# Four transformer layers and two conditioned ones on one core: attention probabilities scaled by the matmul that turns them, and the turned banks copied by two engines

## The chip, the cores and the metric

The kernel runs on one core of one Trainium2 chip. Times are device microseconds (us) of one execution. TensorE appears in the rows as two lines, PE for matmuls and PEld for the loading of their stationary operand; VectorE is DVE, ScalarE is ACT, SyncE is SP.

## The reference

A sequence of 256 tokens of width 1024 goes through four layers (mixers: NSA, MoBA, a short convolution, NSA; each followed by a gated feed-forward) and then through two more layers of another kind (MLA and neighbourhood attention). All in float32. The part that matters here is masked softmax attention with 16 heads of 64:

```python
def masked_softmax(s, mask):
    s = jnp.where(mask, s.astype(jnp.float32), -jnp.inf)
    m = jnp.max(s, axis=-1, keepdims=True)
    m = jnp.where(jnp.isfinite(m), m, 0.0)
    e = jnp.where(mask, jnp.exp(s - m), 0.0)
    d = jnp.sum(e, axis=-1, keepdims=True)
    return e / jnp.where(d > 0, d, 1.0)
...
o = (gates[:, :, 0, :, :, None] * o_cmp + gates[:, :, 1, :, :, None] * o_slc
     + gates[:, :, 2, :, :, None] * o_win).astype(h.dtype)
```

In NSA each head has a compressed, a selected and a window branch, each multiplied by a gate per token and head. With 256 tokens the selected and the window branch are both plain causal attention. MoBA is plain causal attention here, without gates.

## The kernel before, in words

Each engine runs its own instruction list, written out stage by stage in the order of `PROGRAM`; engines meet only at semaphores. Three stages use `pair_attention` with causal masks: `nsa0` and `nsa1` (16 items each: 8 tiles of two heads, times two branches) and `moba0` (8 items). A fourth, `na0`, uses the same function with 512 wide rows. An item is two heads (e = 0, 1), each with 256 query tokens in two blocks: 128 queries against 128 keys, and 128 queries against 256 keys. So a head has 384 columns (`WIDTH`), an item 768.

What one item goes through, with the engine that does it:

- scores: PE, L482, stationary and moving operand from `qk`, heads e = 0 and 1 in the two halves of the rows of the array (64 partitions each); semaphore `s_ready`.
- mask and row maximum: DVE, L2197, four instructions from `ps` to `p_pair` (part of `hid_f`); `s_taken`.
- exp with row sum: ACT, L1385, four instructions in place; `exp_done`.
- `normalize`: DVE, reciprocal of the four sums (L2172), in NSA times the gate (L2176), then the four blocks of `p_pair` times their factor (L2182); `p_ready`.
- turning: PE, L801, 12 transposes of half a block each (64 queries by 128 keys), again in the two halves of the rows, into the two banks `PAIR_T` = 4 and 5, one for each half r; `t_ready`.
- copy to `t_pair`: ACT, L1398, one instruction over both banks; `t_taken`.
- product with the values: PE, L818, stationary `v_sb`, moving `t_pair`; in NSA the first branch of a tile also takes the compressed branch from `v_sb` (its own scores and scaling are made elsewhere); `pv_done`.
- after a tile's last item: ACT (L1405) and DVE (L1792) split the result into `a_both`.

PE's list in round i of the loop holds scores(i), the turning of item i-2, the value product of item i-3. DVE's holds the maximum of item i, `normalize` of item i-1, the split of item i-4. ACT's holds exp of item i, the copy of item i-1, the split of item i-3. There is one pair of banks `PAIR_T`: the turning of an item waits until the item before it has been copied out. In the last rounds PE fills in parts of the output projection (`out_part`) around the last two turnings.

Of the kernel before, what the change touches and what calls it, by code (L numbers as in the profile page):

```python
# [13 lines left out]
P = 128  # L14
# [3 lines left out]
HD = 64  # L18
# [113 lines left out]
def program(nc, weights, small, x_t, c_rows, ctx_t, na_bias, na_bv, out_t):  # L132
    with ExitStack() as ctx:
# [4 lines left out]
        def sb(name, shape, dt=F32):  # L138
            return ctx.enter_context(nc.sbuf_tensor(name, shape, dt))
# [37 lines left out]
        low_stat = sb("low_stat", [P, 2, 4])  # L177
        cmp_max = sb("cmp_max", [P, 2 * HEADS])
        cmp_sum = sb("cmp_sum", [P, 2 * HEADS])

        q_sb, k_sb = qk[:, 0:KD], qk[:, KD:2 * KD]
        sq_sum = p_ring[:, 0, 0:S]
# [60 lines left out]
        def wait(eng, s, n):  # L243

            if n > 0:
                eng.wait_ge(s, n)
# [126 lines left out]
        p_slot = [hid_f32[0][:, 2 * S * j:2 * S * (j + 1)] for j in range(4)]  # L373
        WIDTH = {"nsa0": 3 * P, "nsa1": 3 * P, "moba0": 3 * P, "na0": 4 * P}
        PAIR_SLOTS = 3

        def p_pair(name, i):

            w = 2 * WIDTH[name]
            at = 0 if name == "na0" else FT * S - PAIR_SLOTS * w  # L380
            return hid_f32[0][:, at + i % PAIR_SLOTS * w:at + (i % PAIR_SLOTS + 1) * w]

        def t_pair(name, i):

            w = 2 * WIDTH[name]
            at = 0 if name == "na0" else FT * S - PAIR_SLOTS * w
            return hid_f32[1][:, at + i % PAIR_SLOTS * w:at + (i % PAIR_SLOTS + 1) * w]

        NEG_SCALE = {"nsa0": -HD ** -0.5, "nsa1": -HD ** -0.5, "moba0": -HD ** -0.5,
                     "mla0": -float(np.float32((NOPE + ROPE) ** -0.5)), "na0": -1.0}  # L390
# [86 lines left out]
        def _(pe):  # L477
# [283 lines left out]
            def pair_attention(name, src, beside):  # L761

                a, items = att[name], ITEMS[name]
                N, W = len(items), WIDTH[name]
                out = {}

                def out_part(tiles):
                    if not out:
                        pe.wait_ge(a["s_taken"], N - 1)
                        out["unit"], out["made"] = start_unit("AA")  # L770
                        for bank, p, _ in out["made"]:
                            start_product("A", p)
                    for k in tiles:
                        pe.wait_ge(a["o_ready"], k + 1)
                        for j, (bank, p, (ready, _)) in enumerate(out["made"]):
                            last = fm_tile(ps[:, bank, 0:S], out["unit"] % SLOTS, j * KD + k, src[k], k == 0, k == KD - 1)
                            if k == KD - 1:
                                last.then_inc(ready, 1)

                wait(pe, taken["A"], cnt.n["A"])  # L780
                for i in range(N + 3):
                    if i < N:
                        if i >= 2:
                            pe.wait_ge(a["s_taken"], i - 1)
                        for c in range(len(items[i]["heads"][0]["scores"])):
                            many = len(items[i]["heads"][0]["scores"][c][1])
                            for t in range(many):
                                for e in range(2):
                                    cols, terms = items[i]["heads"][e]["scores"][c]
                                    last = mm(ps[:, PAIR_S[i % 2][e], cols], *terms[t], t == 0, t == many - 1)  # L790
                        last.then_inc(a["s_ready"], 1)
                    beside(i)
                    if i == N:
                        out_part(range(0, 3))
                    b = i - 2
                    if 0 <= b < N:
                        pe.wait_ge(a["p_ready"], b + 1)
                        wait(pe, a["t_taken"], b)
                        for at in range(0, 2 * W, P):
                            for r in range(2):  # L800
                                last = nc.tensor.transpose(ps[:, PAIR_T[r], at // 2:at // 2 + HD], p_pair(name, b)[half(r), at:at + P],  # L801
                                                           ident[half(r), half(r)])
                        last.then_inc(a["t_ready"], 1)
                    if i == N + 1:
                        out_part(range(3, 5))
                    b = i - 3
                    if 0 <= b < N:
                        it = items[b]
                        o = PAIR_O[it["tile"] % 2]
                        pe.wait_ge(a["t_taken"], b + 1)  # L810
                        if it["tile"] >= 2:
                            pe.wait_ge(a["o_ready"], it["tile"] - 1)
                        many = len(it["heads"][0]["pv"])
                        for j in range(many):
                            for e in range(2):
                                v, t, q = it["heads"][e]["pv"][j]
                                moving = t_pair(name, b)[:, e * W + t.start:e * W + t.stop] if isinstance(t, slice) else t
                                last = nc.tensor.matmul(ps[half(e), o, q], v, moving, start=it["first"] and j == 0,  # L818
                                                        stop=j == many - 1, skip_group_check=True)
                        last.then_inc(a["pv_done"], 1)  # L820
                out_part(range(5, KD))
# [349 lines left out]
        def _(act):  # L1171
# [201 lines left out]
            def pair_attention(name, beside=None, behind=None, load_bias=None):  # L1373

                a, items = att[name], ITEMS[name]
                N, W = len(items), WIDTH[name]
                for i in range(N + 3):
                    if i < N:
                        act.wait_ge(a["s_taken"], i + 1)
                        rows = items[i]["rows"]  # L1380
                        for e in range(2):
                            for r, (c, _) in enumerate(rows):
                                at = p_pair(name, i)[:, e * W + c.start:e * W + c.stop]
                                x = len(rows) * e + r
                                last = nc.scalar.activation(at, at, ACT.Exp, bias=negmax[:, i % 4, x:x + 1], scale=-1.0,  # L1385
                                                            accum_out=sums[:, i % 4, x:x + 1])
                        last.then_inc(a["exp_done"], 1)
                        if load_bias and i + 2 < N:
                            load_bias(i + 2)
                    if beside:  # L1390
                        beside(i)
                    b = i - 1
                    if 0 <= b < N:
                        act.wait_ge(a["t_ready"], b + 1)
                        if b >= PAIR_SLOTS:
                            act.wait_ge(a["pv_done"], b - PAIR_SLOTS + 1)
                        turned = ps[:, PAIR_T[0]:PAIR_T[1] + 1, 0:W].rearrange("p r (n c) -> p r n c", c=HD)
                        nc.scalar.copy(t_pair(name, b).rearrange("p (n r c) -> p r n c", r=2, c=HD), turned).then_inc(a["t_taken"], 1)  # L1398
                    if behind:
                        behind(i)  # L1400
                    b = i - 3
                    if 0 <= b and items[b]["last"]:
                        act.wait_ge(a["pv_done"], b + 1)
                        t = items[b]["tile"]
                        nc.scalar.copy(a_hi[:, t, LAT], ps[:, PAIR_O[t % 2], 0:S]).then_inc(a["o_hi"], 1)  # L1405
# [372 lines left out]
        def _(dve):  # L1778
# [383 lines left out]
            def pair_attention(name, out_unit, beside=None, bias=False):  # L2162
# [4 lines left out]
                def normalize(b):  # L2167
# [5 lines left out]
                    if g is not None:  # L2173
                        sync()
                        both = recip[:, b % 4, :].rearrange("p (e r) -> p e r", e=2)
                        step(v.tensor_tensor(both, both, gate[:, :, g:g + REP + 1:REP].rearrange("p r e -> p e r"), ALU.mult))  # L2176
                    sync()
                    for e in range(2):
                        for r, (c, _) in enumerate(rows):
                            at = p_pair(name, b)[:, e * W + c.start:e * W + c.stop]  # L2180
                            x = len(rows) * e + r
                            last = v.tensor_scalar(at, at, recip[:, b % 4, x:x + 1], None, ALU.mult)  # L2182
                    last.then_inc(a["p_ready"], 1)

                for i in range(N + 4):
# [18 lines left out]
                        normalize(1)  # L2204
                    if beside:
                        beside(i)
                    b = i - 4
                    if 0 <= b and items[b]["last"]:
                        tiles += 1
# [53 lines left out]
            def run_nsa(j):  # L2263
                s = nsa[j]
                if cnt.n["unit"] == 0:
# [8 lines left out]
                        add_square()  # L2274
                    dve.wait_ge(rest_loaded, 16)
                    split(1)
                norm_row()
                v_rep = [h.rearrange("p (m g r c) -> p m g r c", m=2, g=GROUPS, r=REP) for h in (vg_hi, vg_lo)]
                blocks = blk_f.rearrange("p (kv l g c) -> p kv l g c", kv=2, l=16, g=GROUPS)
# [735 lines left out]
```

## Time and profile before

| | |
|---|---|
| median of 3 runs | 2270.99 us (2268.38 to 2271.54) |
| the profiled execution's own time | 2267.76 us |
| its span in the trace | 2266.0 us |
| granted TensorE clock, mean | 0.993 |
| PE busy | 2211.7 us (98%) |
| DVE busy | 1786.1 us (79%) |
| ACT busy | 1161.0 us (51%) |

The span runs from the first to the last instruction in the trace; the own time holds 1.8 us around it. A granted clock of 1.00 is 2.4 GHz, 0.50 is 1.2 GHz. Busy shares are means over stages that differ much: the three stages in question take about 0.1 ms of the 2.27.

### The profile page before, as it was taken

The numbers are of one execution on the slowest core, as the hardware profiler recorded it, in microseconds if no ns is written. First come the engines' busy times: TensorE is split into PE (matmuls) and PEld (weight loads), VectorE is DVE, ScalarE is ACT, GpSimd is POOL, SyncE is SP. The second block draws the span as 40 slices with busy tenths as digits, with TensorE's granted clock in tenths as the row PEclk, the third lists the DMA queues.
The fourth block names the chain that finished last, engine by engine and source line by source line (L and its number), as shares of the span: only waits on it lengthen the run. The fifth ranks groups of instructions, "written<-read, shape, count | busy, mean of one in ns | idle before, by whom it ended". The sixth has DMA issues, their size and how long they took to land.

```text
span 2266.0 us, 38094 instructions
## 1 busy us (share of the span) xinstructions
PE 2211.7 (98%) x15324; PEld 1975.1 (87%) x15324; DVE 1786.1 (79%) x3510; ACT 1161.0 (51%) x2042; POOL 0.2 (0%) x4
## 2 busy tenths in 40 slices
PE   7999999999999999999999999999999999999998
PEld 7878889898889988897988887788888889979998
DVE  7788977789887898878798866577877876478888
ACT  4685554665553555458655634534122235476433
POOL 0000000000000000000000000000000000000000
PEclk9999999999999999999999999999999999999999
DMA  7325656356555565650565532023454522334563
GB/s 247 135 71 218 234 198 220 122 196 235 197 209 187 195 234 197 214 207 30 205 232 200 181 112 93 1 75 130 167 187 157 176 75 103 140 104 149 207 227 125
DMA packets 70160, 373.60 MB, mean 165 GB/s; under 512 B 7392, under 2 KB 16736, under 8 KB 37984
## 3 DMA queue, kind: packets, MB, share of 16 engines
q1 hardware_dynamic: 61472, 361.52, 44.4%
q10 hardware_dynamic: 8512, 9.63, 1.4%
q8 instruction: 122, 2.00, 0.3%
q14 instruction: 54, 0.44, 0.1%
HBM read 369.03 MB, written 1.05 MB: 163 GB/s over the span
## 4 chain that ended last, share of the span: by engine, by line
PE 83%; DVE 10%; ACT 3%; DMA 2%; issue 1%; DVEq 0%; ACTq 0%
PE ps L482 80%; DVE w_lo L1792 3%; DMA w_raw<-weights 1%; DVE hid_f L2197 1%; DVE hid_f L2182 1%; PE ps L818 1%; PE ps L735 1%; ACT w_hi L1183 1%; PE ps L801 1%; ACT hid_f L1385 1%; DMA sm<-small 1%; DVE v_sb L2297 0%; DVE ps L1826 0%; DVE hid_both L1792 0%; DVE a_both L1792 0%
## 5 line engine op out<-in xcount | busy, mean ns | idle before, releaser
L482 PE MATMUL ps<-a_both,w_hi 128*128 128x256 f32 (+1 forms) x4864 | 1187.2, 330 | 16.2 <-DVE a_both L1849 10.4
L482 PEld LDWEIGHTS ps<-a_both,w_hi 128*128 128x128 f32 x4864 | 808.5, 190 | 93.5 <-issue 15.2
L482 PE MATMUL ps<-a_both,w_lo 128*128 128x256 f32 (+1 forms) x3136 | 886.2, 291 | 0.0
L1792 DVE TENSOR_TENSOR w_lo<-w_raw,w_hi 128x1024 fp32r<-128x1024 f32 (+1 forms) x632 | 707.4, 1147 | 83.8 <-ACT w_hi L1183 77.0
L482 PEld LDWEIGHTS ps<-a_both,w_lo 128*128 128x128 f32 x3136 | 595.4, 190 | 26.5
L482 PE MATMUL ps<-hid_both,w_hi 128*128 128x512 f32 (+2 forms) x2216 | 600.5, 350 | 6.2 <-DVE hid_both L1792 2.3
L1183 ACT CAST w_hi<-w_raw 128x1024 fp32r<-128x1024 f32 (+1 forms) x448 | 414.7, 974 | 369.8 <-DMA w_raw<-weights 369.0
L482 PEld LDWEIGHTS ps<-hid_both,w_hi 128*128 128x128 f32 x2216 | 385.8, 189 | 63.9 <-issue 4.6
L482 PE MATMUL ps<-hid_both,w_lo 128*128 128x256 f32 (+2 forms) x1460 | 438.4, 304 | 0.0
L482 PEld LDWEIGHTS ps<-hid_both,w_lo 128*128 128x128 f32 x1460 | 276.5, 189 | 14.3
L1189 ACT CAST w_hi<-w_raw 128x1024 fp32r<-128x1024 f32 (+2 forms) x184 | 187.8, 1021 | 1.2 <-DMA w_raw<-weights 1.2
L1826 DVE CUSTOM_DVE_ANT_1 ps<-pe_sb,X 128x1024 f32<-128x1024 f32 x104 | 127.8, 1229 | 1.8
L1548 ACT COPY p_ring<-ps 128x512 f32<-128x512 f32 x88 | 51.7, 587 | 140.0 <-PE ps L482 135.7
L1205 ACT ACTIVATE p_ring<-ps 128x512 f32<-128x512 f32 (+1 forms) x56 | 28.2, 505 | 166.9 <-PE ps L482 166.6
L1826 DVE CUSTOM_DVE_ANT_0 ps<-pe_sb,c_late 128x1024 f32<-128x1024 f32 x88 | 108.2, 1230 | 3.2
L1385 ACT ACTIVATE hid_f<-hid_f,negmax 128x128 f32<-128x128 f32 (+1 forms) x192 | 94.1, 499 | 14.1 <-DVE negmax L2197 14.1
L482 PE MATMUL ps<-w_hi,a_both 128*128 128x256 f32 x512 | 95.8, 289 | 0.0
L2490 DVE TENSOR_TENSOR p_ring<-ps,p_ring 128x512 f32<-128x512 f32 x88 | 60.6, 689 | 42.3 <-ACT p_ring L1548 42.3
L482 PEld LDWEIGHTS ps<-w_hi,a_both 128*128 128x128 f32 x512 | 81.6, 196 | 2.9 <-issue 2.5
L1792 DVE TENSOR_TENSOR hid_both<-t_ring,hid_both 128x256 fp32r<-128x256 f32 (+1 forms) x152 | 72.2, 477 | 3.2 <-ACT hid_both L1694 1.3
L482 PE MATMUL ps<-w_lo,a_both 128*128 128x256 f32 x256 | 73.3, 286 | 0.0
L1551 ACT ACTIVATE p_ring<-p_ring 128x256 f32<-128x256 f32 x88 | 36.8, 419 | 54.7 <-DVE p_ring L2492 54.6
(235 smaller groups left out, 1907.3 us busy)
## 6 DMA issues: line engine op xcount, KB each, us to landing
w_raw<-weights SPq DMA_DIRECT2D x250, 1024.0 KB, 4.6
pe_sb<-weights SPq DMA_DIRECT2D x96, 512.0 KB, 5.4
w_raw<-weights SPq DMA_DIRECT2D x64, 704.0 KB, 3.8
pe_sb<-na_bias ACTq DMA_DIRECT2D x32, 128.0 KB, 2.2
X<-x_t SPq DMA_DIRECT2D x2, 512.0 KB, 6.8
X<-c_rows ACTq DMA_DIRECT2D x2, 512.0 KB, 4.4
qk<-qk ACTq DMA_DIRECT2D x4, 256.0 KB, 6.8
qk<-ctx_t ACTq DMA_DIRECT2D x1, 1024.0 KB, 5.7
```

The source lines that it names most:

```text
L482: return nc.tensor.matmul(out, stationary, moving, start=start, stop=stop)
L735: last = nc.tensor.matmul(ps[:, o, q], v, t_ring[:, e, t], start=j == 0, stop=j == len(it["pv"]) - 1, skip_group_check=True)
L801: last = nc.tensor.transpose(ps[:, PAIR_T[r], at // 2:at // 2 + HD], p_pair(name, b)[half(r), at:at + P], ident[half(r), half(r)])
L1183: nc.scalar.copy(w_hi[:, u % SLOTS, c], raw(u, c)).then_inc(hi_split, 1)
L1189: nc.scalar.copy(w_hi[:, u % SLOTS, c], raw(u, c)).then_inc(hi_split, 1)
L1205: nc.scalar.activation(dst, src, func or ACT.Copy, **kw).then_inc(taken[ring], 1)
L1385: last = nc.scalar.activation(at, at, ACT.Exp, bias=negmax[:, i % 4, x:x + 1], scale=-1.0, accum_out=sums[:, i % 4, x:x + 1])
L1548: nc.scalar.copy(low_slot, ps[:, at, S:2 * S]).then_inc(low_copied, 1)
L1551: nc.scalar.activation(gate_sum, gate_sum, ACT.Silu).then_inc(silu_done, 1)
L1792: return v.tensor_tensor(out, a, b.bitcast(F32), ALU.subtract)
L1826: v.tensor_tensor_reduce(products, ada_w[:, a % 2, :].rearrange("p (a b) -> p a b", b=S), c, 1.0, 0.0, ALU.mult, ALU.add, mod[:, a, s_:s_ ...
L2490: v.tensor_tensor(both, ps[:, made[0][0]:made[1][0] + 1, 0:S], low_slot, ALU.add).then_inc(taken["A"], 1)
```

## The change

For `nsa0`, `nsa1` and `moba0` (not for `na0` and `mla0`) DVE no longer multiplies the probabilities by their factors. It writes four 64 by 64 diagonal matrices, one for each block of the item, into `factor` (a view of `t_ring`, four items deep), and PE multiplies by these in place of the identity: `nc.tensor.transpose` with `ident` becomes an ordinary float32 `matmul` with `factor` as the moving operand. `ident_half` holds the two diagonal blocks of the identity side by side as one 128 by 64 tile and is made once, at the start. The copy out of `PAIR_T` is split: ACT takes bank 4, DVE takes bank 5, and `t_taken` counts two for each item.

```diff
+        ident_half = sb("ident_half", [P, HD])
...
+        SCALED_TURN = ("nsa0", "nsa1", "moba0")
+        factor = t_ring.rearrange("p a (b x c) -> p (a b) x c", b=2, c=HD)
+
+        def copies(name):
+            return 2 if name in SCALED_TURN else 1
...
+        def turned(name, i, halves_of):
+
+            tokens = t_pair(name, i).rearrange("p (n r c) -> p r n c", r=2, c=HD)[:, halves_of]
+            first = PAIR_T[0] + halves_of.start
+            return tokens, ps[:, first:first + halves_of.stop - halves_of.start, 0:WIDTH[name]].rearrange("p r (n c) -> p r n c", c=HD)
...
                         pe.wait_ge(a["p_ready"], b + 1)
-                        wait(pe, a["t_taken"], b)
+                        wait(pe, a["t_taken"], copies(name) * b)
                         for at in range(0, 2 * W, P):
+                            x = 2 * (at // W) + (at % W > 0)
                             for r in range(2):
-                                last = nc.tensor.transpose(ps[:, PAIR_T[r], at // 2:at // 2 + HD], p_pair(name, b)[half(r), at:at + P],
-                                                           ident[half(r), half(r)])
+                                to, frm = ps[:, PAIR_T[r], at // 2:at // 2 + HD], p_pair(name, b)[half(r), at:at + P]
+                                if name in SCALED_TURN:
+                                    last = mm(to, frm, factor[half(r), b % 4, x, :], True, True)
+                                else:
+                                    last = nc.tensor.transpose(to, frm, ident[half(r), half(r)])
...
-                        turned = ps[:, PAIR_T[0]:PAIR_T[1] + 1, 0:W].rearrange("p r (n c) -> p r n c", c=HD)
-                        nc.scalar.copy(t_pair(name, b).rearrange("p (n r c) -> p r n c", r=2, c=HD), turned).then_inc(a["t_taken"], 1)
+                        nc.scalar.copy(*turned(name, b, slice(0, 3 - copies(name)))).then_inc(a["t_taken"], 1)
...
                     sync()
+                    if name in SCALED_TURN:
+                        v.tensor_tensor(factor[:, b % 4], ident_half[:, :].unsqueeze(1).to_broadcast([P, w, HD]),
+                                        recip[:, b % 4, 0:w].unsqueeze(2).to_broadcast([P, w, HD]), ALU.mult).then_inc(a["p_ready"], 1)
+                        return
...
+                    b = i - 2
+                    if name in SCALED_TURN and 0 <= b < N:
+                        dve.wait_ge(a["t_ready"], b + 1)
+                        if b >= PAIR_SLOTS:
+                            dve.wait_ge(a["pv_done"], b - PAIR_SLOTS + 1)
+                        v.tensor_copy(*turned(name, b, slice(1, 2))).then_inc(a["t_taken"], 1)
```

On PE, in the first rounds of `nsa0`, before the change (`sm` holds `ident`, `hid_f` is `p_pair`; an x12 row is one item's turning):

```order
L482 MATMUL ps<-qk 128x128 x2
L482 MATMUL ps<-qk 128x256 x2
L801 MATMUL ps<-sm,hid_f_0_50 128x64 x12
L818 MATMUL ps<-hid_f_1_51,v_sb 64x256 x2
L818 MATMUL ps<-hid_f_1_51,v_sb 64x128 x2
```

and after it, where the number, the shapes and the order of the matmuls are the same, and the moving operand of the twelve is `t_ring` (`factor`):

```order
L494 MATMUL ps<-qk 128x128 x2
L494 MATMUL ps<-qk 128x256 x2
L494 MATMUL ps<-t_ring,hid_f_0_50 128x64 x12
L834 MATMUL ps<-hid_f_1_51,v_sb 64x256 x2
L834 MATMUL ps<-hid_f_1_51,v_sb 64x128 x2
```

On DVE, in the same rounds of `nsa0`, before the change:

```order
L2172 RECIPROCAL recip<-sums 128x4
L2176 TENSOR_TENSOR recip<-recip,gate 128x4
L2182 TENSOR_SCALAR hid_f_0_50<-hid_f_0_50,recip 128x128
L2182 TENSOR_SCALAR hid_f_0_50<-hid_f_0_50,recip 128x256
L2182 TENSOR_SCALAR hid_f_0_50<-hid_f_0_50,recip 128x128
L2182 TENSOR_SCALAR hid_f_0_50<-hid_f_0_50,recip 128x256
L2197 ISA hid_f_0_50,negmax<-ps,sm 128x128
```

and after it, where one wide product stands in place of the four scalings, and behind it the copy of the item before (`ps` bank 5 to `t_pair`), ahead of the next item's maximum:

```order
L2187 RECIPROCAL recip<-sums 128x4
L2191 TENSOR_TENSOR recip<-recip,gate 128x4
L2194 TENSOR_TENSOR t_ring<-ident_half,recip 128x256
L2231 COPY hid_f_1_51<-ps 128x6x64
L2216 ISA hid_f_0_50,negmax<-ps,sm 128x128
```

## Rows read from the trace of the kernel before

**Rows 1.** The page: busy time of the engines, and the longest chain by line.

```profile
PE 2211.7 (98%) x15324; PEld 1975.1 (87%) x15324; DVE 1786.1 (79%) x3510; ACT 1161.0 (51%) x2042; POOL 0.2 (0%) x4
PE ps L482 80%; DVE w_lo L1792 3%; DMA w_raw<-weights 1%; DVE hid_f L2197 1%; DVE hid_f L2182 1%; PE ps L818 1%; PE ps L735 1%; ACT w_hi L1183 1%; PE ps L801 1%; ACT hid_f L1385 1%; DMA sm<-small 1%; DVE v_sb L2297 0%; DVE ps L1826 0%; DVE hid_both L1792 0%; DVE a_both L1792 0%
```

**Rows 2.** Window, `nsa0`: length; PE, PEld, DVE, ACT, POOL busy; PEclk; DMA.

```profile
122.76:128.08 5.32, 4.71 (x64) 3.23 (x61) 5.17 (x30) 5.28 (x21) 0.00 (x0) 1.00 0.03 6
```

**Rows 3.** Timeline of PEld, `nsa0`: start, length (us), instruction, [idle before <-releaser].

```profile
130.94 0.45 PEld L801 LDWEIGHTS ps<-sm,hid_f 64*128 64x128 f32 x12 [1.01 <-DVE hid_f L2182]
131.46 0.20 PEld L818 LDWEIGHTS ps<-v_sb 128*64 128x64 f32 x4
...
132.69 0.52 PEld L482 LDWEIGHTS ps<-qk 64*128 64x128 f32 x8 [0.17 <-issue]
133.38 0.46 PEld L801 LDWEIGHTS ps<-sm,hid_f 64*128 64x128 f32 x12 [0.17 <-DVE hid_f L2182]
133.91 0.63 PEld L818 LDWEIGHTS ps<-hid_f,v_sb 128*64 128x64 f32 x8
134.71 0.52 PEld L482 LDWEIGHTS ps<-qk 64*128 64x128 f32 x8 [0.17 <-issue]
136.25 0.46 PEld L801 LDWEIGHTS ps<-sm,hid_f 64*128 64x128 f32 x12 [1.02 <-DVE hid_f L2182]
```

**Rows 4.** Timeline of DVE, `nsa0`, from one item's normalisation to the next item.

```profile
131.91 0.17 DVE L2172 RECIPROCAL recip<-sums 128x4 f32<-128x4 f32 x1
...
132.32 1.01 DVE L2182 TENSOR_SCALAR hid_f<-hid_f,recip 128x128 f32<-128x128 f32 x4
133.24 0.42 DVE L1792 TENSOR_TENSOR a_both<-ps,a_both 128x256 fp32r<-128x256 f32 x1
```

**Rows 5.** Groups of instructions by form, DVE and ACT: busy us, mean ns.

```profile
L2492 DVE TENSOR_TENSOR p_ring<-p_ring,r_row 128x256 f32<-128x256 f32 x88 | 37.4, 425 | 3.0
L2758 DVE COPY qk<-ps 128x512 f32<-128x512 f32 x8 | 5.5, 688 | 6.5 <-PE ps L482 6.5
L1398 ACT COPY hid_f<-ps 128x768 f32<-128x768 f32 x40 | 31.6, 791 | 6.9 <-PE ps L801 6.6
L1548 ACT COPY p_ring<-ps 128x512 f32<-128x512 f32 x88 | 51.7, 587 | 140.0 <-PE ps L482 135.7 <-issue 4.4
```

**Rows 6.** PEld: L801 by source; L482 by form; a timeline stretch before `nsa0`.

```profile
L801 PEld LDWEIGHTS ps<-sm,hid_f x736: 134/139/227, 101.8 to 2036.7; 64*128 64x128 f32 x184
...
L482 PEld LDWEIGHTS ps<-qk 64*128 64x128 f32 x320 | 22.2, 196 | 5.9 <-issue 4.8
...
85.81 2.87 PEld L482 LDWEIGHTS ps<-k_cmp,qk 128*128 128x128 f32 x25
```

**Rows 7.** Timeline of PEld: third turning and start of `out_part`, `nsa0`, `nsa1`, `moba0`.

```profile
107.25 0.45 PEld L801 LDWEIGHTS ps<-sm,hid_f 64*128 64x128 f32 x12 [1.47 <-DVE hid_f L2182]
...
138.01 0.30 PEld L482 LDWEIGHTS ps<-a_both,w_hi 128*128 128x128 f32 x2 [0.17 <-issue]
...
1040.45 0.45 PEld L801 LDWEIGHTS ps<-sm,hid_f 64*128 64x128 f32 x12 [1.47 <-DVE hid_f L2182]
...
1071.20 0.30 PEld L482 LDWEIGHTS ps<-a_both,w_hi 128*128 128x128 f32 x2 [0.17 <-issue]
...
435.62 0.45 PEld L801 LDWEIGHTS ps<-sm,hid_f 64*128 64x128 f32 x12 [2.21 <-DVE hid_f L2182]
...
445.20 0.30 PEld L482 LDWEIGHTS ps<-a_both,w_hi 128*128 128x128 f32 x2 [0.17 <-issue]
```

**Rows 8.** Windows, `moba0` and behind the compressed scores; a turning in `moba0`.

```profile
434.00:436.00 2.00, 0.38 (x12) 0.38 (x12) 1.62 (x8) 2.00 (x8) 0.00 (x0) 1.00 0.00 0
...
438.00:440.00 2.00, 2.00 (x20) 1.37 (x18) 1.67 (x12) 2.00 (x9) 0.00 (x0) 0.50 0.04 8
...
90.00:92.00 2.00, 2.00 (x10) 1.28 (x11) 1.93 (x7) 1.54 (x2) 0.00 (x0) 0.50 0.00 0
...
438.07 0.98 PEld L801 LDWEIGHTS ps<-sm,hid_f 64*128 64x128 f32 x12 [0.20 <-DVE hid_f L2182]
```

More of the change, by code:

```diff
@@ L809, in pair_attention @@
                         o = PAIR_O[it["tile"] % 2]
-                        pe.wait_ge(a["t_taken"], b + 1)
+                        pe.wait_ge(a["t_taken"], copies(name) * (b + 1))
                         if it["tile"] >= 2:
@@ L2276, in run_nsa @@
                     split(1)
+                    step(v.tensor_tensor(ident_half[:, :], ident[:, 0:HD], ident[:, HD:P], ALU.add))
                 norm_row()
```

## The prediction

> **What bounds the kernel now.** I read the page first. PE is busy 98% of the span and the chain of waits lies on its line L482 for 80% [rows 1], so whatever lengthens PE's list outside a wait lengthens the kernel; the change can gain only where PE waits. The causal attention stages are such places. The windows over one tile of `nsa0` (two items) show why: of 5.32 us ACT is busy 5.28, DVE 5.17, PE by its records 4.71, and PEld 3.23 [rows 2]. DVE and ACT set the pace together there, and PE waits for DVE's scaling.
>
> The timeline of PEld shows how much. I measure a group from its first weight load to the first load of the next group. A turning takes 131.46 − 130.94 = 0.52 us, a value product with the compressed branch 132.69 − 131.46 = 1.23, one without 134.71 − 133.91 = 0.80, an item's scores 133.38 − 132.69 = 0.69 [rows 3]. Two items are 2 × 0.69 + 2 × 0.52 + 1.23 + 0.80 = 4.45 us of PE's list. The tile takes 136.25 − 130.94 = 5.31 [rows 3], so PE waits 0.86 a tile, 0.43 an item. That is all the room the turning has to grow in before PE sets the pace.
>
> **What DVE and ACT save.** Before, DVE's four scalings hold it from 132.32 to 133.24, 0.92 us [rows 4]. In their place stands one product of 128x256: 425 ns in the nearest row [rows 5], some 0.35 if the next instruction starts inside its tail, as DVE's do here (four scalings of 1.01 us in all let the next begin after 0.92). New is the copy of one bank, 384 columns: a DVE copy of 512 takes 688 ns, and 256 columns take 425 in the product above, halfway 0.55 [rows 5], about 0.48 with the tail overlapped. DVE: 0.92 − 0.83 = 0.09 us less an item. ACT's copy of 768 columns takes 791 ns and one of 512 takes 587 [rows 5]; 0.8 ns a column makes 0.48 for 384, so ACT saves 0.31 an item. `ident_half` costs one 64 wide DVE instruction at the start, at most 0.3 us, beside PE's matmuls on loaded weights. If PE had kept its turning at 0.52, DVE's saving would be the whole gain: 40 items × 0.09 = 3.6 us.
>
> **What PE pays.** The twelve turnings are now ordinary float32 matmuls, and the trace has none that loads 64 rows by 128 columns and streams 64 columns, so I price it by neighbours. A transpose leaves one record (40 items × 12 + 16 × 16 = 736, and L801 has x736), with a load of 139 ns [rows 6]. A float32 matmul leaves two: 40 items × 4 score matmuls are 160, and the rows show x320, with loads of 196 ns [rows 6]. So there are twice the passes, each with a longer load. The distance between passes: in the transposes six pairs (the two row halves run side by side) start within 0.45 − 0.14 us, 0.062 a pair. In the scores four pairs start their loads within 0.52 − 0.19, 0.11 a pair [rows 3, 6]. Those stream 128 and 256 columns, so the 0.11 might be streaming; but the compressed scores stream only 32 columns per 128x128 load, and 25 of their loads take 2.87 us, (2.87 − 0.19) / 24 = 0.112 apart [rows 6]. So a float32 pass costs 0.112 us when little is streamed: the load sets it. The item now has 12 pairs instead of 6: first load to last load grows from 0.31 to 11 × 0.112 = 1.23, so the turning goes from 0.52 to **1.44 us, +0.92**, over twice the 0.43 that PE has free.
>
> In the Trainium skill, TensorE: Matmul & The Clock Gate, section Terms, the transpose mode is said to be 4 times faster for float32. Four times the 0.31 us between first and last load would be 1.24; the page speaks against this change as my rows do, by the same size.
>
> Bounds of the turning. Below: 24 loads at the transposes' spacing, 12 × 0.062, would make +0.37. Above: if the two halves no longer ran side by side, 24 × 0.112 would make +2.2. The scores have the same operand type and the same halves, and run side by side; I take 0.92.
>
> **The sum.** With 1.44 a tile of NSA is 2 × 0.69 + 2 × 1.44 + 2.03 = 6.29 us of PE's list, against 4.97 to 5.15 of DVE and 4.7 of ACT: PE sets the pace and waits for nobody. From the third turning to `out_part` there were 138.01 − 107.25 = 30.76 us in `nsa0` and 1071.20 − 1040.45 = 30.75 in `nsa1` [rows 7]. PE's list in it: 12 turnings, 6 + 6 value products, 11 scores. That is 12 × 1.44 + 6 × 2.03 + 11 × 0.69 = 37.05, **+6.3**. The first two turnings add 1.84, of which the 1.47 us wait before the third [rows 7] takes up most: **+0.4**. The last two stand between full projection matmuls: 2 × 0.92 = **+1.8**. Each NSA stage +8.5, two of them +17.0.
>
> `moba0` has 8 items and no compressed branch: from the third turning to `out_part` 445.20 − 435.62 = 9.58 us [rows 7], and afterwards 4 × 1.44 + 4 × 0.80 + 3 × 0.69 = 11.03, +1.45. The 2.21 us wait before the third turning [rows 7] hides the first two. The last two add 1.84. Together **+3.3**. In the old trace the clock fell to 1.2 GHz here after PE had been busy 0.38 of 2 us [rows 8]; with longer turnings that gap nearly closes, so I count full clock; 9.58 includes what the fall cost.
>
> Sum: 17.0 + 3.3 = +20.3. Nothing later takes it back, since PE is the bound in the stages behind [rows 1]. Against the profiled execution's 2267.76 this is 2288.1; against the median of the runs shown (2270.99) it is 2291.3. I say **2290**, own range 2284 to 2298.
>
> **The rivals.**
>
> *The turning is cheap (ends on the other side).* If the passes of these 64 column matmuls kept the transposes' spacing of 0.062, a turning would be 0.89 and PE's tile 5.19 against DVE's 5.15. The whole effect in the steady part is then DVE's −0.09 an item, and the first rounds lose the 0.6 us by which `p_ready` comes earlier: at best −3.6 − 1.5 = −5, 2263 to 2266. It decides at a turning of (5.31 − 3.41) / 2 = 0.95 us: above that PE is slower than the old pace. For it speaks only that no row has just this shape; against it the spacing of 0.112 with 32 columns. Chance 0.04 for faster by over 0.2% (4.5 us, about what a measurement can tell from no change), 0.06 for no difference.
>
> *Both copies are late.* A turning now waits for ACT's and DVE's copy of the item before, and DVE's stands behind `normalize`. From the start of a turning: scores visible after 0.2, maximum of four blocks about 1.2, reciprocal and gate 0.4 (131.91 to 132.32 [rows 4]), factors 0.42, copy 0.55: 2.8 us. PE comes back to the next turning after 1.44 + 0.80 + 0.69 = 2.93. A margin of 0.15 in the items without compressed branch; if something in it is 0.3 longer, some 20 items wait 0.2 to 0.3: +5, 2295. Chance 0.13.
>
> *The clock falls.* In the rows of `moba0` the fall came after idling, and at 0.50 the loads of a turning spread over 0.98 us instead of 0.45 [rows 3, 8]. The new turning keeps the array loaded but streams in half the time only. Should a fall of 4 us, as in `moba0`, come once in each stage, it costs 2 us each, 2296; if the clock stays at 1.2 GHz through the three stages, 40 items cost some 3 us more each, 2400. For it: the clock is also at 0.50 at 90 us, right behind the compressed scores with their many loads and little streaming, though PE was busy throughout [rows 6, 8]. Against: PE's share of streaming an item hardly changes, since 0.43 of wait is replaced by 0.92 of half streaming. Chance 0.13, mostly for the small form. By the Trainium skill (the same page, Part 4: PE-mode transpose) transposes do not count as busy time for the clock; by that rule the clock in `moba0` would stay up.
>
> *Mine,* PE pays 0.92 a turning: 0.64.
>
> **How the numbers follow.** The upper rivals up to 2300 or so are taken in; below I go to where the turning costs 0.6 more in place of 0.92 (20 − 40 × 0.3 = +8). Range 2278 to 2306. Slower by over 0.2%: 0.64 + 0.13 + 0.13 = 0.90; same 0.06; faster 0.04.
>
> **What the new profile would show.** Twice the records of the turnings (960 beside 256 transposes), loads near 190 ns, 1.4 to 1.5 us from the first load to the next group; tiles of NSA 6.3 us apart; PE's idle before turnings near nothing; DVE and ACT idle some 1 us a tile, waiting for PE's scores. `out_part` of `nsa0` starts 6 to 7 us later than 138.01. I am wrong if the turnings take under 0.95, if PE still idles before them for DVE's copy, or if the windows of the three stages show a clock below 1.00 where it was 1.00.

## The result and the profile after

The changed kernel takes 2292.93 us (median of 4 runs, 2292.10 to 2293.59), the kernel before 2271.26 (4 runs, 2268.38 to 2271.81): a ratio of 1.0097, 95% interval 1.0085 to 1.0109. It is slower by 21.7 us. The profiled execution took 2292.41, with a span of 2290.3 (before 2267.76 and 2266.0).

The page after, busy time and the longest chain by line, beside [rows 1] (L494 is the matmul helper that was L482, L834 the value product that was L818):

```profile
PE 2246.6 (98%) x15804; PEld 2016.7 (88%) x15804; DVE 1785.0 (78%) x3431; ACT 1150.9 (50%) x2042; POOL 0.2 (0%) x4
PE ps L494 83%; DVE w_lo L1807 3%; PE ps L834 2%; DMA w_raw<-weights 2%; PE ps L747 1%; ACT w_hi L1199 1%; DMA sm<-small 1%; PE ps L818 0%; DVE v_sb L2323 0%; DVE hid_both L1807 0%; DVE X L1933 0%; PE ps L735 0%; DVE X L2080 0%; ACT p_ring L1337 0%; DVE X L1929 0%
```

PE has 480 records and 35 us more, DVE 79 instructions less. Of DVE's lines in the stages, L2182 and L2197 in the chain before, none stands in it now. Over one tile of `nsa0`, two items (the window's columns are those of [rows 2]):

```profile
120.86:127.17 6.31, 6.31 (x86) 5.31 (x84) 5.03 (x28) 4.74 (x19) 0.00 (x0) 1.00 0.01 3
```

The tile takes 6.31 us instead of 5.32, PE is busy in all of it, and DVE and ACT are both below their old 5.17 and 5.28. PEld's timeline over a tile shows what the time goes to, beside [rows 3]:

```profile
128.95 1.52 PEld L494 LDWEIGHTS ps<-t_ring,hid_f 64*128 64x128 f32 x24
130.54 0.63 PEld L834 LDWEIGHTS ps<-hid_f,v_sb 128*64 128x64 f32 x8
131.34 0.52 PEld L494 LDWEIGHTS ps<-qk 64*128 64x128 f32 x8 [0.17 <-issue]
131.91 1.50 PEld L494 LDWEIGHTS ps<-t_ring,hid_f 64*128 64x128 f32 x24
133.48 0.20 PEld L834 LDWEIGHTS ps<-v_sb 128*64 128x64 f32 x4
133.75 0.79 PEld L834 LDWEIGHTS ps<-hid_f,v_sb 128*64 128x64 f32 x8
134.72 0.52 PEld L494 LDWEIGHTS ps<-qk 64*128 64x128 f32 x8 [0.17 <-issue]
```

A turning has 24 loads in place of 12 and takes 1.59 and 1.57 us to the next group; the value products stand at 0.80 and 1.24 as before; the scores take 0.57. No row of the tile waits for DVE or ACT. Groups by form (busy us, mean ns | idle before and its releaser), beside [rows 5, 6]:

```profile
L494 PEld LDWEIGHTS ps<-t_ring,hid_f 64*128 64x128 f32 x960 | 59.4, 188 | 4.5 <-issue 2.7
L2231 DVE COPY hid_f<-ps 128x384 f32<-128x384 f32 x40 | 22.1, 553 | 6.2 <-PE ps L494 6.0
L1413 ACT COPY hid_f<-ps 128x384 f32<-128x384 f32 x40 | 19.1, 478 | 38.3 <-PE ps L494 38.2
L2194 DVE TENSOR_TENSOR t_ring<-ident_half,recip 128x256 f32<-128x256 f32 x40 | 17.0, 425 | 1.4
```

And the waits from 110 to 147 us (us in total, times, longest): now the other engines wait for PE.

```profile
ACT hid_f L1413 <- PE ps L494: 9.7, 12, 1.1
DVE hid_f L2216 <- PE ps L494: 7.1, 12, 0.8
```

The third turning, `out_part` and the last two turnings of `nsa0`, and the third turning and `out_part` of `moba0`, beside [rows 7]:

```profile
110.01 1.52 PEld L494 LDWEIGHTS ps<-t_ring,hid_f 64*128 64x128 f32 x24
...
147.34 0.30 PEld L494 LDWEIGHTS ps<-a_both,w_hi 128*128 128x128 f32 x2 [0.17 <-issue]
...
149.68 1.42 PEld L494 LDWEIGHTS ps<-t_ring,hid_f 64*128 64x128 f32 x24
151.17 0.63 PEld L834 LDWEIGHTS ps<-hid_f,v_sb 128*64 128x64 f32 x8
151.97 1.44 PEld L494 LDWEIGHTS ps<-t_ring,hid_f 64*128 64x128 f32 x24 [0.17 <-issue]
...
446.49 0.29 PEld L494 LDWEIGHTS ps<-t_ring,hid_f 64*128 64x128 f32 x3 [0.40 <-issue]
...
457.63 0.30 PEld L494 LDWEIGHTS ps<-a_both,w_hi 128*128 128x128 f32 x2 [0.17 <-issue]
```

From the third turning to `out_part` `nsa0` took 37.33 us (30.76 before) and `moba0` 11.14 (9.58). From the first matmul of a stage's first turning to its last value product, by the trace's records, the stages `nsa0`, `moba0`, `nsa1` went from 43.76, 22.78, 43.75 to 52.23, 26.09, 52.29: +8.47, +3.31, +8.54, together **+20.3 us**. I call this difference the stage sum below. It is read from one execution of each kernel.

### The profile page after: what moved, and what is told of

Same layout as the page of the kernel before. It is cut to its first block, busy times and chain, and to the rows that moved or that the text cites. A ratio compares the mean times of both kernels' runs of the same rounds, so it can differ in the third digit from the quotient of the medians.

```text
span 2290.3 us, 39006 instructions
## 1 busy us (share of the span) xinstructions
PE 2246.6 (98%) x15804; PEld 2016.7 (88%) x15804; DVE 1785.0 (78%) x3431; ACT 1150.9 (50%) x2042; POOL 0.2 (0%) x4
## 4 chain that ended last, share of the span: by engine, by line
PE 87%; DVE 7%; DMA 3%; ACT 3%; issue 1%; ACTq 0%; DVEq 0%
PE ps L494 83%; DVE w_lo L1807 3%; PE ps L834 2%; DMA w_raw<-weights 2%; PE ps L747 1%; ACT w_hi L1199 1%; DMA sm<-small 1%; PE ps L818 0%; DVE v_sb L2323 0%; DVE hid_both L1807 0%; DVE X L1933 0%; PE ps L735 0%; DVE X L2080 0%; ACT p_ring L1337 0%; DVE X L1929 0%
## 5 line engine op out<-in xcount | busy, mean ns | idle before, releaser
L494 PE MATMUL ps<-a_both,w_hi 128*128 128x256 f32 (+1 forms) x4864 | 1188.2, 330 | 18.4 <-DVE a_both L1864 10.5
L494 PEld LDWEIGHTS ps<-a_both,w_hi 128*128 128x128 f32 x4864 | 808.9, 190 | 96.3 <-issue 15.3
L494 PE MATMUL ps<-a_both,w_lo 128*128 128x256 f32 (+1 forms) x3136 | 886.4, 291 | 0.0
L494 PEld LDWEIGHTS ps<-a_both,w_lo 128*128 128x128 f32 x3136 | 595.8, 190 | 26.5
L494 PE MATMUL ps<-hid_both,w_hi 128*128 128x512 f32 (+2 forms) x2216 | 602.3, 351 | 6.0 <-DVE hid_both L1807 2.3
L494 PEld LDWEIGHTS ps<-hid_both,w_hi 128*128 128x128 f32 x2216 | 387.1, 190 | 64.1 <-issue 4.6
L494 PE MATMUL ps<-hid_both,w_lo 128*128 128x256 f32 (+2 forms) x1460 | 439.1, 304 | 0.0
L494 PEld LDWEIGHTS ps<-hid_both,w_lo 128*128 128x128 f32 x1460 | 277.2, 190 | 14.3
L494 PE MATMUL ps<-w_hi,a_both 128*128 128x256 f32 x512 | 95.8, 289 | 0.0
L494 PEld LDWEIGHTS ps<-w_hi,a_both 128*128 128x128 f32 x512 | 81.7, 196 | 2.9 <-issue 2.5
L494 PE MATMUL ps<-w_lo,a_both 128*128 128x256 f32 x256 | 73.3, 286 | 0.0
```

The costliest lines, as they stand in the source:

```text
L494: return nc.tensor.matmul(out, stationary, moving, start=start, stop=stop)
```

## Why the spans differ by 4 us more than the stages

The spans differ by 24.3. Part of the rest is there before the change can act: the first turning of `nsa0` starts at 104.33 instead of 101.77. The windows ahead of it, of the changed kernel:

```profile
86.00:88.00 2.00, 2.00 (x14) 1.91 (x13) 0.00 (x0) 1.21 (x3) 0.00 (x0) 0.67 0.36 53
88.00:90.00 2.00, 2.00 (x11) 2.00 (x11) 1.75 (x2) 1.16 (x2) 0.00 (x0) 0.50 0.88 344
```

And of the kernel before:

```profile
86.00:88.00 2.00, 2.00 (x20) 2.00 (x19) 0.62 (x1) 2.00 (x4) 0.00 (x0) 1.00 0.72 205
88.00:90.00 2.00, 2.00 (x15) 2.00 (x14) 2.00 (x3) 0.29 (x1) 0.00 (x0) 0.69 0.76 320
```

The granted clock falls to 0.50 in the compressed scores in both, in one execution about 2 us earlier. That is scatter and not the change: e9 and e12 below are one and the same kernel, and their first turnings start at 103.93 and 102.00. The other experiments that have PE's instructions of before up to this point start at 101.96 (e3), 102.11 (e8) and 103.75 (e2).

Another 1.5 us comes behind the three stages. The same group of loads stands at 2066.02 us before and at 2088.82 after, 22.8 later; right behind it the changed kernel's trace has the clock down, where the kernel before has 1.00, and from there on it is 24.3 behind:

```profile
2066.02 0.97 PEld L482 LDWEIGHTS ps<-sm,p_ring 128*128 128x128 f32 x8 [0.53 <-issue]
...
2088.82 0.97 PEld L494 LDWEIGHTS ps<-sm,p_ring 128*128 128x128 f32 x8 [0.53 <-issue]
...
2090.00:2092.00 2.00, 2.00 (x11) 1.95 (x11) 1.94 (x2) 0.98 (x2) 0.00 (x0) 0.57 0.04 8
```

The trace of e3 has this fall too and that of e1 has not, so it doesn't go with the turning's mode either. The medians differ by 21.7, so 1.4 us beyond the stage sum are left, which is within that scatter.

## The experiments

Each is compared with the kernel before, run beside it on the same chip (2271.5 us for e1 to e4, 2271.9 for e5 to e7, 2271.25 for e8 to e11); stage sums are differences from the one trace of the kernel before. T is a turning in `nsa0`, first load to the next group's.

**e1: the mode alone.** Only the instruction of the turning is changed in the kernel before; scaling and copy stay.

```diff
-    last = nc.tensor.transpose(ps[...], p_pair(name, b)[half(r), at:at + P], ident[half(r), half(r)])
+    to, frm = ps[...], p_pair(name, b)[half(r), at:at + P]
+    if name != "na0":
+        last = mm(to, frm, ident[half(r), half(r)], True, True)
+    else:
+        last = nc.tensor.transpose(to, frm, ident[half(r), half(r)])
```

> The kernel before, with the transposes of the three causal stages replaced by ordinary float32 matmuls by the same identity; DVE scales and ACT copies both banks as before. If the passes on PE are the whole cost: turning 1.5 to 1.6 us, NSA tiles 6.3 us apart, +20 us (2291), within 3 us of the changed kernel. If the cost came from the copy behind normalize in DVE's list or from the factors, this kernel stays within 4 us of the kernel before.

Measured 2294.38 against 2271.5, 1.0103 (1.0089 to 1.0117). PEld's timeline of e1:

```profile
121.69 1.52 PEld L482 LDWEIGHTS ps<-sm,hid_f 64*128 64x128 f32 x24
123.28 0.63 PEld L821 LDWEIGHTS ps<-hid_f,v_sb 128*64 128x64 f32 x8
...
128.00 0.19 PEld L482 LDWEIGHTS ps<-sm,hid_f 64*128 64x128 f32 x2
```

The tile is again 128.00 − 121.69 = 6.31 and the stage sum +21.8. The whole cost is the mode of twelve instructions an item. Diagonal and second copy add nothing to it; by the stage sums they take off 1.5 us, which the two medians can't tell.

**e2: transposes, twice.** In the kernel before the twelve transposes of an item are issued twice (the same result again): T grows without the mode.

```diff
+    if name != "na0":
+        for at in range(0, 2 * W, P):
+            for r in range(2):
+                to, frm = ps[...], p_pair(name, b)[half(r), at:at + P]
+                last = nc.tensor.transpose(to, frm, ident[half(r), half(r)])
```

> The kernel before, with each item of the three stages turned twice over into the same banks by transposes. As many array passes as in the changed kernel, at the transposes' spacing of 0.062 us a pair: turning 0.52 + 0.37 = 0.89, PE's tile 5.19, under DVE's and ACT's 5.3. If PE's wait of 0.43 an item is free room: nothing in the steady part, 2 x 0.37 us at the end of each stage, +2 us (2273). If the number of passes counts, not the load of each: +20. If the cost is simply additive on PE: 40 x 0.37 = +15.

Measured 2277.86, 1.0030 (1.0019 to 1.0041), stage sum +6.8: the 2273 that I gave for free room was too low, and the +15 of a plain addition too high. The timeline of e2 over one tile shows why (PE's, DVE's and PEld's rows that matter; L2202 is the maximum, L2187 the scaling, L802 and L807 the two halves of the turning):

```profile
125.18 0.52 PEld L482 LDWEIGHTS ps<-qk 64*128 64x128 f32 x8 [0.17 <-issue]
...
126.15 0.29 DVE L2202 CUSTOM_DVE_ANT_0 hid_f<-ps,sm 128x128 f32<-128x128 f32 x1 [0.39 <-PE ps L482]
...
127.68 1.01 DVE L2187 TENSOR_SCALAR hid_f<-hid_f,recip 128x128 f32<-128x128 f32 x4
...
128.74 0.45 PEld L802 LDWEIGHTS ps<-sm,hid_f 64*128 64x128 f32 x12 [0.63 <-DVE hid_f L2187]
...
129.63 0.20 PEld L823 LDWEIGHTS ps<-v_sb 128*64 128x64 f32 x4
...
130.86 0.52 PEld L482 LDWEIGHTS ps<-qk 64*128 64x128 f32 x8 [0.17 <-issue]
```

DVE waits for PE's scores, and PE then waits for DVE's scaling, which stands behind that maximum. That is a loop over the engines. It takes two items, one tile, to come round: the scores of item i release its maximum; behind this in DVE's list stands the scaling of item i − 1, which releases that item's turning; behind the turning in PE's list come the value product of item i − 2, with the compressed branch, and the scores of item i + 2. In the rows: scores to maximum 126.15 − 125.18 = 0.97, maximum to turning 128.74 − 126.15 = 2.59, the turning 0.89, value product with the compressed branch 130.86 − 129.63 = 1.23; together 5.68. Only one of the tile's two turnings is in it. Without the turning it is **4.79 + T**, and with the old T of 0.52 that is 5.31, the tile of before. The sum from scores to scores is the tile by construction; that the rest stays at 4.79 while T changes, and that the loop can be cut, is what e3 and e8 have to show.

**e3: half the turning as plain matmuls.**

```diff
+    if name != "na0" and at < W:
+        last = mm(to, frm, ident[half(r), half(r)], True, True)
```

> The kernel before, with head e = 0 turned by ordinary float32 matmuls by the identity and head e = 1 by transposes: half the dose. Turning 0.52 + 6 x 0.112 - 3 x 0.062 = 1.01, PE's tile 5.43 against 5.31. With free room of 0.43 an item: +0.06 an item in NSA, nothing steady in MoBA, 2 x 0.49 at the end of each stage: +4.5 us (2276). A cost in proportion to the dose: +10 (2281).

Measured 2280.39, 1.0044 (1.0031 to 1.0056), stage sum +9.0, where a cost in proportion to the dose was foreseen at +10 and free room at +4.5. PEld's timeline of e3 (L805 is the half left as transposes):

```profile
121.52 0.75 PEld L482 LDWEIGHTS ps<-sm,hid_f 64*128 64x128 f32 x12 [0.57 <-DVE hid_f L2185]
...
127.31 0.75 PEld L482 LDWEIGHTS ps<-sm,hid_f 64*128 64x128 f32 x12 [0.58 <-DVE hid_f L2185]
127.92 0.33 PEld L805 LDWEIGHTS ps<-sm,hid_f 64*128 64x128 f32 x6
128.32 0.20 PEld L821 LDWEIGHTS ps<-v_sb 128*64 128x64 f32 x4
```

T is 1.01, the tile 5.79; 4.79 + 1.01 is 5.80. PE still waits 0.57 a tile for DVE, though the tile has grown: the wait was not free room.

**e4: the changed kernel, transposes again.** Factors and second copy stay, but the turning doesn't apply the factors, so the probabilities are left unscaled.

```diff
-    last = mm(to, frm, factor[half(r), b % 4, x, :], True, True)
+    last = nc.tensor.transpose(to, frm, ident[half(r), half(r)])
```

> The changed kernel, with the transposes by the identity put back; DVE still writes the factors, which nobody uses, so the probabilities stay unscaled, and both engines copy a bank each. It gives what the change would save if turning cost nothing more. From the sum: DVE -0.09 an item and the first rounds shorter, -4 to -5 us (2266). If splitting the copy brings waits of its own (both copies late), it is at or above the kernel before.

Measured 2267.21, 0.9983 (0.9974 to 0.9992), stage sum −3.4. DVE's saving is real, by the interval 2 to 6 us. The NSA stages gain 0.7 each, in their first rounds, `moba0` 2.0. In `moba0` part of this can be the clock: only the trace of the kernel before has it at 0.50 there. PEld's timeline of e4:

```profile
122.46 0.48 PEld L816 LDWEIGHTS ps<-sm,hid_f 64*128 64x128 f32 x12 [0.95 <-DVE t_ring L2194]
123.01 0.20 PEld L834 LDWEIGHTS ps<-v_sb 128*64 128x64 f32 x4
...
127.75 0.48 PEld L816 LDWEIGHTS ps<-sm,hid_f 64*128 64x128 f32 x12 [0.95 <-DVE t_ring L2194]
```

The tile is still 5.29: PE now waits for the product that makes the factors, which has the scaling's place in the loop, with a T of 0.55 in the waiting item.

**e5: the second copy without the rest.** The kernel before, with the turned ones copied in two halves as after (ACT bank 4, DVE bank 5), but the scaling on DVE and the transposes as before.

```diff
+    b = i - 2
+    if name in SCALED_TURN and 0 <= b < N:
+        dve.wait_ge(a["t_ready"], b + 1)
...
+        v.tensor_copy(*turned(name, b, slice(1, 2))).then_inc(a["t_taken"], 1)
```

> The kernel before, with only the copy split: ACT bank 4, DVE bank 5, scalings left on DVE and transposes as before. DVE's tile goes from 5.17 to 5.17 + 2 x 0.48 = 6.13 us: +0.4 an item, +14 to +17 us (2286). If DVE had room in its list, or if ACT's shorter copy set the pace, no change or a gain.

Measured 2281.57, 1.0044 (1.0032 to 1.0056), stage sum +10.7. The tile was foreseen at 5.17 + 2 × 0.48 = 6.13 and is 128.19 − 122.06:

```profile
122.06 0.48 PEld L812 LDWEIGHTS ps<-sm,hid_f 64*128 64x128 f32 x12 [0.60 <-DVE hid_f L2192]
...
125.29 0.48 PEld L812 LDWEIGHTS ps<-sm,hid_f 64*128 64x128 f32 x12 [1.36 <-DVE hid_f L2192]
...
128.19 0.23 PEld L812 LDWEIGHTS ps<-sm,hid_f 64*128 64x128 f32 x4 [0.60 <-DVE hid_f L2192]
```

DVE's list is nearly full in that tile (5.99 of 6.13 us busy). The total, 2286, was foreseen too high, as I counted all 40 items at that pace; of the 16 turnings of an NSA stage only the 12 between the third and `out_part`, six tiles, run at it (6 × 0.82 = 4.9, and the stage grew by 4.9).

**e6: the changed kernel with both copies on ACT.**

```diff
-    return 2 if name in SCALED_TURN else 1
+    return 1
...
-    if name in SCALED_TURN and 0 <= b < N:
+    if copies(name) == 2 and 0 <= b < N:
```

> The changed kernel, with ACT copying both banks as before. If PE's list is the whole bound, the same as the changed kernel within 2 us, NSA tiles 6.3 us apart. If DVE's copy just before the next turning holds PE back, this is 3 to 5 us faster than the changed kernel.

Measured 2294.89 against 2271.9, 1.0100 (1.0087 to 1.0113). The tile is 6.32 by the turnings at 120.42 and 126.74, the stage sum +21.3. DVE rid of its copy changes nothing, so no late copy sets the pace. In the changed kernel itself DVE's copy is done only 0.11 us before PE's next turning at 131.91 (timeline of DVE):

```profile
130.90 0.42 DVE L2194 TENSOR_TENSOR t_ring<-ident_half,recip 128x256 f32<-128x256 f32 x1
131.25 0.55 DVE L2231 COPY hid_f<-ps 128x384 f32<-128x384 f32 x1
```

**e7: the turning in one pass.** Probabilities and factors are rounded to fp32r, so the turning has 12 loads again.

```diff
-    last = mm(to, frm, factor[half(r), b % 4, x, :], True, True)
+    last = mm(to, p_pair_r(name, b)[half(r), at:at + P], factor[half(r), b % 4, x, :], True, True)
```

> The changed kernel, with probabilities and factors written as fp32r and turned by fp32r matmuls: both are rounded, so the output is less exact. One pass for each matmul at the load spacing of 0.112: turning 0.52 + 5 x 0.05 = 0.77 us, PE's tile 4.95, under the threshold of 5.3. If the second pass is what costs, the kernel is back at the pace of DVE and ACT, 2266 to 2271. If the ordinary matmul as such (no transpose mode) costs, it stays over 2285.

Measured 2275.17 against 2271.9, 1.0018 (1.0009 to 1.0028), stage sum +3.0 (+1.83, −0.75, +1.95); I had expected a gain or none, or over 2285. The twelve executions lie between 2270.64 and 2281.02, and the four above 2278 have the lowest granted clocks (0.991 and 0.992, the others 0.993 to 0.995), so the median may hold some of that; the stage sum is from an execution of 2272.37 with 0.994. PEld's timeline of e7:

```profile
123.69 0.77 PEld L500 LDWEIGHTS ps<-t_ring_r,hid_both 64*128 64x128 f32 x12 [0.74 <-DVE t_ring_r L2201]
124.51 0.20 PEld L840 LDWEIGHTS ps<-v_sb 128*64 128x64 f32 x4
...
129.25 0.77 PEld L500 LDWEIGHTS ps<-t_ring_r,hid_both 64*128 64x128 f32 x12 [0.74 <-DVE t_ring_r L2201]
```

T is 0.82 (0.77 foreseen), below the 0.95 at which the prediction had it decide, and yet the tile grows to 5.56, because PE waits for the factors. In e4 the tile is 5.29 with a T of 0.55 in the waiting item, 4.74 + T; here 4.74 + 0.82 = 5.56.

**e8 to e12: the value product out of the loop.** If the loop is the cause, it must shrink when PE issues the scores of item i + 1 behind the turning of item i − 2 and ahead of the value product of item i − 3. This was done to e3 (e8), the kernel before (e9), the changed one (e10) and e4 (e11, unscaled like e4).

```diff
     for i in range(N + 3):
-        if i < N:
-            ... scores of item i ...
+        if i < N and (not early or i <= 3):
+            scores(i)
...
         last.then_inc(a["t_ready"], 1)
+        if early and 3 <= i < N - 1:
+            scores(i + 1)
```

> The half dose kernel (e3), with PE's list changed from the fourth round on: the scores of item i+1 stand ahead of the value product of item i-3, not behind it. New theory: a loop through scaling, turning, value product with compressed branch, scores, maximum and scaling again sets the tile at 4.79 + T, T being one turning; it takes the value product's 1.23 us out of the loop, so the tile falls from 5.80 to the longest list, PE's 5.3 to 5.4, and the time by 5 to 6 us (2275). First theory (only PE's list against free waits): PE's list is unchanged, so no change from e3 (2280).

> The kernel before with the same reordering of PE's list. Loop theory: the loop (5.31) goes, but ACT's list of 5.28 a tile stays: within 2 us of the kernel before. If the loop was not at work, also no change; if scores held ahead of the value product delay something else, slower.

> The changed kernel with the same reordering. Its tiles of 6.31 are PE's list, which is unchanged: within 2 us of the changed kernel (2293). If its tile came from the loop (4.75 + 1.58 = 6.33, the same number by chance), it would fall by up to 1.2 a tile, over 10 us in all.

> The kernel with the transposes put back and factors unused (e4, probabilities unscaled) with the same reordering. Loop theory: the tile of 5.28, which was the loop (4.75 + 0.52), falls to DVE's list of 5.0: 3 to 4 us faster than e4 (2263). If e4's tile was a list of DVE or ACT, no change.

The window over one tile of e8:

```profile
122.74:128.20 5.46, 5.46 (x74) 4.02 (x73) 5.17 (x30) 5.34 (x20) 0.00 (x0) 1.00 0.01 3
```

Of e9:

```profile
118.31:123.52 5.21, 4.56 (x62) 3.05 (x60) 5.07 (x30) 5.21 (x20) 0.00 (x0) 1.00 0.00 0
```

Of e10:

```profile
120.30:126.72 6.42, 6.42 (x86) 4.99 (x84) 5.29 (x25) 4.73 (x20) 0.00 (x0) 1.00 0.01 3
```

Of e11:

```profile
120.60:125.58 4.98, 4.56 (x62) 3.08 (x60) 4.84 (x26) 4.81 (x20) 0.00 (x0) 1.00 0.02 5
```

e8 goes from 5.79 to 5.46 with PE busy throughout; e9 from 5.31 to 5.21, where ACT is full; e11 from 5.29 to 4.98, where no engine is full. Nothing was taken from any engine's work. e10, where PE is full already, gains nothing (6.42). The times: e8 2277.20, 1.0026 (1.0015 to 1.0036), e3 had 1.0044; e9 2269.15, 0.9992 (0.9983 to 1.0001); e10 2290.87, 1.0087 (1.0073 to 1.0100); e11 2264.19, 0.9968 (0.9956 to 0.9981), e4 had 0.9983. By the stage sums e8 took back 3.3 us of e3's 9.0, all of it in the NSA stages (5 to 6 were foreseen), and e11 is 3.5 better than e4 (3 to 4 foreseen). The tiles carry the case here: the intervals of e8 and e3, and of e11 and e4, overlap.

> The same kernel as e9, the kernel before with the scores of item i+1 ahead of the value product of item i-3, a second time, since its first ratio (0.9992) was as large as its interval. Its tiles in the trace were 5.21 us against 5.31, which over some 6 tiles in each NSA stage and MoBA is 1 to 2 us. If the tiles tell the truth: ratio 0.999 to 0.9995 again. If the first result was chance: at or above 1.

e12 is e9 once more: 2268.45 against 2269.74, 0.9996 (0.9987 to 1.0005). Both intervals of the reordered kernel before hold 1, so it isn't shown to be faster. The stage sum is −1.2 us both times, less than these medians can tell.

## Why the prediction was right, and which step was not

**What bounds the kernel.** Right in that PE's list becomes the bound after the change: window, waits and e10 show it, and e6 shows that DVE's copy is not what sets the pace.

**What DVE and ACT save.** The product takes 425 ns and DVE's copy 553, as read from the neighbours; ACT's copy 478 against 480. `ident_half` is one instruction of 220 ns at 18.3 us, for which nobody waited. e4 gives the saving as 3.4 us of stage sum (3.6 foreseen), but that the two agree is luck: it comes in the first rounds and in `moba0`, there perhaps in part from the clock, and not as 0.09 an item. The NSA tile only goes from 5.31 to 5.29.

**What PE pays.** The turning was foreseen at 1.44 and the scores at 0.69; they are 1.57 to 1.59 and 0.54 to 0.57, and the sum of the two, 2.13, is what was said. The cut between the groups lies elsewhere, as the old scores row was followed by a wait. The tile came out at 6.31 (6.29). The loads take 188 ns at a spacing of (1.42 − 0.19) / 11 = 0.112 in the last turnings, so the price by the load was right, and by e1 it is the mode that costs. By the Trainium skill (TensorE: Matmul & The Clock Gate, section Terms) the transpose mode is 4 times faster for float32; the trace agrees, with 0.31 us before and 1.42 − 0.19 = 1.23 in the last turnings after, from a turning's first load to its last.

**The sum.** NSA +8.47 and +8.54 (8.5 each), MoBA +3.31 (3.3): the +20.3 of the prediction. That it fits to the tenth is luck. `nsa0` from the third turning to `out_part` grew by 6.57 (6.3 foreseen), the first two turnings and the last two by 1.90 together (2.2), and these misses cancel; the same twelve plain matmuls an item gave +21.8 in e1 and +21.3 in e6. The measured 2292.93 lies 2.9 above the 2290 that I gave, of which 1.3 is my rounding down from 2291.3.

**The rivals.** Late copies: margin foreseen 0.15, found 0.11 in `nsa0`; e6 excludes them as a cost, as it is no faster without DVE's copy. The clock: 1.00 in the tile above, and 1.00 in `moba0`, where it had fallen to 0.50 [rows 8]. The prediction put that fall down to PE's idling ahead of it, and counted full clock because the gap closes. The count came true, the reason isn't shown: in e5, which keeps the transposes, PE is idle in `moba0` for a whole window, and the clock stays at 1.00 there and behind. The windows of `moba0` in the changed kernel and in e5:

```profile
446.00:448.00 2.00, 1.97 (x30) 1.53 (x26) 1.80 (x11) 1.36 (x6) 0.00 (x0) 1.00 0.02 4
...
438.00:440.00 2.00, 0.00 (x0) 0.03 (x1) 2.00 (x14) 1.27 (x4) 0.00 (x0) 1.00 0.98 414
```

**The step that was wrong** is "PE waits 0.86 a tile, 0.43 an item. That is all the room the turning has to grow in before PE sets the pace", and with it the rival's "It decides at a turning of (5.31 − 3.41) / 2 = 0.95 us". There was no room. Before, three things end together at 5.3: ACT's work (5.28), DVE's (5.17) and the loop, 4.79 + 0.52 = 5.31. PE's wait was inside the loop, so every 0.1 of turning is 0.1 a tile at once, until PE's own list is longer: with the 3.41 of the prediction 2T + 3.41 = 4.79 + T at T = 1.38. e2 (0.89), e3 (1.01) and e7 (0.82) lie on the loop. The change lies where loop and list meet: at its T of 1.58, which holds some of what the scores had before, the loop would be 4.74 + 1.58 = 6.32 (4.74 from e4) and PE's list is the measured 6.31. That PE is busy throughout, and that e10 doesn't fall, say that the list is enough to set it. So both readings give the same tile there, and that is why the number held, by luck in this respect; at any T from 0.52 to 1.38 the reading from the list alone would have been too low, as it was in e2 and e3. It also made the rival of the cheap turning too rosy: with T = 0.89 the tile would have been about 4.74 + 0.89 = 5.63, longer than before, not 5.19 (e7 with 0.82 was slower by 3.3 us, not faster); only a turning left near 0.52 gains (e4, 2 to 6 us).

What stays open: how much of DVE's and of ACT's own list still limits the tile of before. e9 says that ACT's does at 5.21; what sets e11's 4.98, with DVE busy 4.84 and ACT 4.81, wasn't followed up; a version that relieves both lists and the loop, with an exact scaling, was not tried.

## What to carry to other kernels

An engine's wait is room only if what it waits for doesn't depend on that engine's own last step: follow the releaser back, and if the path returns to the waiting engine, add up the loop beside each engine's list. In such a loop change the order (here, issue the scores ahead of the value product) before making any step cheaper. Moving arithmetic into a matmul's operand is not free where the matmul replaces a float32 transpose: count the weight loads. Their spacing was 0.112 us both for 128x128 loads with 32 streamed columns (the prediction's neighbour) and for pairs of 64x128 loads with 64 streamed columns, so the neighbour that was bound by its loads gave the right price.

## What the runs showed of the hardware that was not expected

- The fall of the granted clock to 0.50 in the compressed scores comes at a different moment from execution to execution of one kernel, though PE is busy throughout, and moves a span by about 2 us (e9 and e12). The fall at 2090 us is in the traces of the changed kernel and of e3 and in none of the others. Two traces should be compared stage by stage.
- In `moba0` the clock fell to 0.50 before and stayed at 1.00 after. By the Trainium skill (TensorE: Matmul & The Clock Gate, Part 4: PE-mode transpose) transposes don't count as busy in the same way. No run here bears out that they made the difference: e2, e4, e5, e9 and e12 keep the transposes, and their clock stays at 1.00 throughout `moba0`, so the fall may be a matter of the execution and not of the kernel.
- An fp32r turning (e7) has 12 loads, six pairs, as the transposes have, but its pairs start (0.77 − 0.19) / 5 = 0.116 us apart against 0.062 in the transposes: fp32r halves the number of passes of float32 and not the price of one.
